# The first gathered token block of a retrieval layer is finished by POOL inside the last quarter of the loop

## What is computed

```python
def peer(h, ...):                       # h: 640 tokens x 1024
    ...                                 # idx, g: 128 chosen experts and gates for each token
    a = gelu(einsum('tkd,td->tk', expert_u[ix], hx))
    return einsum('tk,tkd->td', gx * a, expert_v[ix])
x = x + g2 * peer(h2, ...)
y = rmsnorm(x, final_g)                 # x * rsqrt(mean(x*x) + EPS) * g
```

## Time and profile before

| | |
|---|---|
| median of 3 runs | 1868.1 us (1866.28 to 1871.09) |
| the profiled execution, its time | 1869.13 us |
| the profiled execution, its span | 1867.3 us |
| PE busy | 1732.7 us (93%) |
| DVE busy | 1519.6 us (81%) |
| POOL busy | 797.7 us (43%) |
| ACT busy | 683.2 us (37%) |

### The profile page before, as it was taken

How to read it: one execution, slowest core, us unless ns; L and a number is a source line. 1 busy time by engine, 2 the same in 40 slices (tenths; PEclk the granted TensorE clock), 3 DMA queues, 4 the chain that set the end, 5 groups by cost and what they waited for, 6 DMA issues and landing times.

```text
span 1867.3 us, 29896 instructions
## 1 busy us (share of the span) xinstructions
PE 1732.7 (93%) x9942; PEld 1483.9 (79%) x9942; DVE 1519.6 (81%) x3123; ACT 683.2 (37%) x1135; POOL 797.7 (43%) x646
## 2 busy tenths in 40 slices
PE   5999988889899998499999999999999999999994
PEld 2667656438788888499999999999999999999994
DVE  0732047245989999999999999999999999999997
ACT  1222146101477674233333333333333333333332
POOL 1111000000000000477877778877666666666661
PEclk8999999899999999699999999999999999999997
DMA  9455100700044555799999999999999999999993
GB/s 358 156 198 221 48 1 1 276 39 12 1 91 91 128 115 134 303 394 405 405 400 387 407 407 407 405 402 399 407 406 397 406 404 399 392 402 407 406 405 135
DMA packets 253543, 520.91 MB, mean 279 GB/s; under 512 B 113955, under 2 KB 130979, under 8 KB 252197
## 3 DMA queue, kind: packets, MB, share of 16 engines
q1 hardware_dynamic: 178016, 249.00, 37.4%
q0 software_dynamic: 73728, 268.47, 36.3%
q10 hardware_dynamic: 1734, 2.60, 0.4%
HBM read 488.55 MB, written 31.46 MB: 278 GB/s over the span
## 4 chain that ended last, share of the span: by engine, by line
PE 53%; DVE 24%; issue 13%; DMA 5%; ACT 3%; DVEq 1%; SPq 0%; POOL 0%; POOLq 0%; PEldq 0%; ACTq 0%
DVE arena L1214 11%; PE ps L1594 9%; PE ps L1593 9%; PE ps L1592 9%; PE ps L1512 5%; PE ps L1493 4%; PE ps L1563 4%; DMA arena_w<-in_w_mod 2%; PE ps L1343 2%; DVE V_lo L1164 2%; PE ps L1347 2%; PE ps L1344 2%; DMA U_in<-in_expert_uT 2%; PE ps L1391 1%; DMA arena_w<-in_w_in 1%
## 5 line engine op out<-in xcount | busy, mean ns | idle before, releaser
L1592 PE MATMUL ps<-hT_hi,U_hi 128*128 128x384 f32 x1024 | 344.3, 336 | 13.6 <-DVE U_lo L1159 13.6
L1594 PE MATMUL ps<-hT_hi,U_lo 128*128 128x384 f32 x1024 | 344.5, 336 | 0.0
L1593 PE MATMUL ps<-hT_lo,U_hi 128*128 128x384 f32 x1024 | 343.7, 336 | 0.0
L1592 PE MATMUL ps<-V_hi,C_hi 128*128 128x512 f32 x768 | 300.5, 391 | 18.1 <-DVE C_lo L1189 18.1
L1593 PE MATMUL ps<-V_lo,C_hi 128*128 128x512 f32 x768 | 302.7, 394 | 0.0
L1594 PE MATMUL ps<-V_hi,C_lo 128*128 128x512 f32 x768 | 302.6, 394 | 0.0
L748 ACT CAST V_hi<-V_in 128x1024 fp32r<-128x1024 f32 x128 | 135.0, 1055 | 217.3 <-PE ps L1594 217.3
L1592 PEld LDWEIGHTS ps<-hT_hi,U_hi 128*128 128x128 f32 x1024 | 193.0, 188 | 18.7 <-issue 13.8
L785 ACT ACTIVATE act_t<-ps 128x384 f32<-128x384 f32 x128 | 63.0, 492 | 393.9 <-PE ps L1594 393.9
L479 POOL DMA_INDIRECT arena<-in_expert_u,idxn x128 | 170.4, 1332 | 85.8 <-issue 32.1
L479 POOL DMA_INDIRECT arena<-in_expert_v,idxn x128 | 159.3, 1244 | 93.4 <-DVE arena L1214 42.8
(11 more groups left out here) (239 smaller groups left out, 3218.8 us busy)
## 6 DMA issues: line engine op xcount, KB each, us to landing
U_in<-in_expert_uT SPq DMA_DIRECT2D x128, 512.0 KB, 9.2
V_in<-in_expert_v SPq DMA_DIRECT2D x128, 512.0 KB, 6.4
arena_w<-in_w_mod SPq DMA_DIRECT2D x12, 2048.0 KB, 12.4
gates_scratch<-arena_w SPq DMA_DIRECT2D x6, 4096.0 KB, 20.8
gate_in<-gates_scratch SPq DMA_DIRECT2D x128, 192.0 KB, 7.4
arena_w<-in_w_in SPq DMA_DIRECT2D x4, 2048.0 KB, 8.9
arena_w<-in_w_query SPq DMA_DIRECT2D x1, 7168.0 KB, 21.1
arena_w<-in_w_out SPq DMA_DIRECT2D x2, 2048.0 KB, 10.4
```

The costliest lines, as they stand in the source:

```text
L1592: nc.tensor.matmul(out, hi, rhi, start=start, stop=False)
L1593: nc.tensor.matmul(out, hi, rlo, start=False, stop=False)
L1594: return nc.tensor.matmul(out, lo, rhi, start=False, stop=stop)
```

## The change

Block 4 is taken out of DVE's tail and given to POOL. POOL's gather loop over the last 128 rows is cut in three (two, two and four turns of sixteen rows). After the first part POOL multiplies `accS[:, 0]` by the gate, after the second it adds it to `XF[:, 4]`, and after the last it does the mean and EPS, the power, and two passes for `XF * rstd` and `* fing`. ACT's Square for that block moves to before the loop's last turn. SP waits for the new `s_yfirst` before it writes block 4 and counts the others by `s_y` as before. DVE's `residual(0)` and `norm3(0)` are gone. On PE the last value sums signal once for each of the three token blocks (`s_vend`), and the residual of block b waits for b of them.

```diff
             for n, b in enumerate(FIN):
-                sp.wait_ge(s_y, n + 1)
+                sp.wait_ge(s_y if n else s_yfirst, max(n, 1))
                 sp.dma_start(y[b * P:(b + 1) * P, :], XF[:, b]).then_inc(s_out, 16)
...
-            for n, (table, k) in enumerate(((expert_u, 1), (expert_v, 0), (expert_v, 1))):
+            for n, (table, k) in enumerate(((expert_u, 1), (expert_v, 0))):
                 with pool.Fori(0, SLOTS // 16) as i:
                     sixteen(table, k, i, (n + 1) * SLOTS // RR)
-            for n, b in enumerate(FIN):
+
+            def last_rows(lo, hi):
+                with pool.Fori(lo, hi) as i:
+                    sixteen(expert_v, 1, i, 3 * SLOTS // RR)
+
+            b0, x0, a0 = FIN[0], XF[:, FIN[0]], accS[:, SPARSE.index(FIN[0])]
+            last_rows(0, 2)
+            pool.wait_ge(s_used, 3 * SLOTS)
+            pool.tensor_tensor(a0, a0, G2[:, min(b0, 1), :], ALU.mult).then_inc(s_first, 1)
+            last_rows(2, 4)
+            pool.wait_ge(s_first, 1)
+            pool.wait_ge(s_xf, 16 * NBLK)
+            pool.tensor_tensor(x0, x0, a0, ALU.add).then_inc(s_x2first, 1)
+            last_rows(4, 8)
+            pool.wait_ge(s_sq3first, 1)
+            pool.tensor_scalar(ss[:, b0:b0 + 1], ss[:, b0:b0 + 1], 1.0 / D, EPS, ALU.mult, ALU.add).then_inc(s_first, 1)
+            pool.wait_ge(s_first, 2)
+            pool.tensor_tensor(rstd[:, b0:b0 + 1], ss[:, b0:b0 + 1], powe[:, 0:1], ALU.pow).then_inc(s_first, 1)
+            pool.wait_ge(s_first, 3)
+            pool.wait_ge(s_fing, 16)
+            pool.tensor_scalar(x0, x0, rstd[:, b0:b0 + 1], None, ALU.mult).then_inc(s_first, 1)
+            pool.wait_ge(s_first, 4)
+            pool.tensor_tensor(x0, x0, fing, ALU.mult).then_inc(s_yfirst, 1)
+            for n, b in enumerate(FIN[1:]):
...
                 experts(i, False, False)
+            act.wait_ge(s_x2first, 1)
+            act.activation(accS[:, SPARSE.index(FIN[0])], XF[:, FIN[0]], ACT.Square,
+                           accum_out=ss[:, FIN[0]:FIN[0] + 1]).then_inc(s_sq3first, 1)
             experts(PAIRS - 1, False, True)
-            for n, b in enumerate(FIN):
+            for n, b in enumerate(FIN[1:]):
...
                 else:
-                    dve.wait_ge(s_v, NB1)
+                    dve.wait_ge(s_vend, b)
                     a = tmp2[b - 1]
...
-            residual(0)
             experts(PAIRS - 1, True, add_row(1))
             residual(1)
-            norm3(0)
             for n in range(2, NBLK):
...
                         last = products3(ps[:, 2 + 2 * b + half, :], C_hi[:, j, tok], C_lo[:, j, tok],
                                          V_hi[:, j, col], V_lo[:, j, col], start, stop)
-                last.then_inc(s_v, 1)
+                    if stop:
+                        last.then_inc(s_vend, 1)
+                if not stop:
+                    last.then_inc(s_v, 1)
```

More of the change, by code:

```diff
@@ L313, in program @@
         s_a = sem("s_a"); s_ge = sem("s_ge"); s_c = sem("s_c"); s_chi = sem("s_chi"); s_clo = sem("s_clo")
-        s_v = sem("s_v"); s_h2out = sem("s_h2out"); s_h2in = sem("s_h2in")
+        s_v = sem("s_v"); s_vend = sem("s_vend"); s_h2out = sem("s_h2out"); s_h2in = sem("s_h2in")
         s_row = [sem(f"s_row{i}") for i in range(RR)]
@@ L317, in program @@
         s_x2 = sem("s_x2"); s_sq3 = sem("s_sq3"); s_var3 = sem("s_var3"); s_rstd3 = sem("s_rstd3"); s_y = sem("s_y")
+        s_first = sem("s_first"); s_x2first = sem("s_x2first"); s_sq3first = sem("s_sq3first"); s_yfirst = sem("s_yfirst")
         s_step = sem("s_step"); s_setp = sem("s_setp")
@@ L1225, in residual @@
                 b = FIN[n]
-                if n == 0:
+                if n == 1:
                     dve.wait_ge(s_xf, 16 * NBLK)
@@ L1242, in norm3 @@
                 b = FIN[n]
-                if n == 0:
+                if n == 1:
                     dve.wait_ge(s_fing, 16)
-                dve.wait_ge(s_sq3, n + 1)
+                dve.wait_ge(s_sq3, n)
                 dve.tensor_scalar(ss[:, b:b + 1], ss[:, b:b + 1], 1.0 / D, EPS, ALU.mult, ALU.add).then_inc(s_var3, 1)
-                dve.wait_ge(s_rstd3, n + 1)
+                dve.wait_ge(s_rstd3, n)
                 dve.scalar_tensor_tensor(out=XF[:, b], in0=XF[:, b], scalar=rstd[:, b:b + 1], in1=fing,
```

## The result

The changed kernel takes 1872.8 us (median of 20 runs, 1869.6 to 1875.5) against 1869.5 us for the kernel before (20 runs beside it, 1865.6 to 1872.3). The ratio is 1.0017, 95% interval 1.0011 to 1.0023: some 3.2 us slower, and within 0.3%. The prediction was +4.4 us, also within 0.3%.

What follows compares the result with a forecast made beforehand. The prediction took DVE to bound the kernel, working through from 1608 us to its end. Terms: -2.40 - 2.03 + 8.8 = +4.4 us, 1872.5 us on the median, with a range of 1863.5 to 1876.5 us.

Steps and rivals of the forecast that it cites:

- What bounds the kernel: From 1608 us DVE works through to the end; PE can fall about 3.0 us behind before DVE waits.
- What is taken out: DVE's tail: block-4 residual, 2.40 us, and norm, 2.03 us, both saved in full, together -4.43 us.
- the signal per block: Before DVE's first PSUM residual: without it about 1.0 us of the norm's 2.03 us would be lost.
- What is added: Four POOL passes, two in the last quarter's loop, two behind the last gather, each stopping DVE 2.2 us: 8.8 us.
- The step that decided: From a 128x8 index copy waiting for a DVE instruction: DVE likely can't begin while POOL reads, so full pass charged.
- the one-input pass: Scaling by rstd on POOL behind the last gather, charged to DVE at the full pass, 2.2 us.
- (a): Rival: the four POOL passes run beside DVE and cost it nothing, 1863.7 us; chance 0.17.
- (b): Rival, same four places: longer passes, 3.1 us each, +8.0 us, 1876.1 us; chance 0.21.
- (c): Rival: DVE's back-to-back instructions shut POOL out until gathered rows run out; DVE waits 10.9 us twice, 1889.9; chance 0.07.
- The gathers' margin: In the quarter: next gather leaves some 2.8 us late, lands by 1643.3, DVE wants it at 1646.3; hidden.
- SP's order: SP waits first for POOL's block 4, done about 1841; DVE's first block about 1854.6, hidden by a dozen us.
- The sum: Whole kernel: -2.40 - 2.03 + 8.8 = +4.4 us, 1872.5 us on the median, 0.24%, within 0.3%.

Runs made afterwards that it cites:

- e2: Changed kernel with only the two loop passes on block 4, its norm left out and its residual written; ratio to the kernel before 1.0006.
- e3: Changed kernel without the two loop passes, so only the block-4 work behind the last gather and ACT's Square; ratio to the kernel before 1.0000.
- e4: Changed kernel with the old signal, one for all last value sums; ratio to the kernel before 1.0024.
- e1: Changed kernel with nothing done for block 4, which is written as loaded; ratio to the kernel before 0.9983.
- e6: Changed kernel with eight more one-input POOL passes, one per turn of the last gather loop; ratio to the kernel before 1.0070.
- e8: Kernel before plus signal per block; block-4 norm off DVE (rstd scaling on ACT, final gain on POOL in halves beside PSUM reads), residual on DVE; ratio 0.9991.
- e9: e8 with DVE's tail reordered, each block's mean one step before its scaling; ratio to the kernel before 0.9974, median 1865.9 us.
- e5: Changed kernel with eight more two-input POOL passes, one per turn of the last gather loop; ratio to the kernel before 1.0114.
- e7: Changed kernel with eight more write-only POOL passes (memset), one per turn of the last gather loop; ratio to the kernel before 1.0018.

## Why the prediction was right

**What bounds the kernel.** Right. DVE set the end: e2, e3 and e4 come out to 0.2 to 0.8 us of Q by adding and taking DVE's times (in e4 its wait for PE) alone, and PE's stalls, in size as foreseen (0.4 us behind the first pass, read from two half-steps that took 8.61 and 8.44 us; 1.8 us and then a fallen clock behind the second), cost nothing. What the prediction didn't say is how near PE is on the other side: e1 lost 0.9 us of its saving to it, through V_hi and V_lo. Nor does DVE work through in all of Q: the wait of 0.7 us for `U_hi` lies near 1603 us, just before the 1608 at which its list of waits began.

**What is taken out.** The 4.43 us were there. Of the signal per block it said that about 1.0 us would be lost without it. With the change in place it is 1.7 us. In e4 PE waits 4.5 us before its last sums, which then take 7.2 us at a granted clock of 0.58, where before it waited 1.9 us and took 6.0 at 0.72; DVE asks 0.5 us later than before, by the wait before the last row, which leaves 1.7.

**What is added.** The step that decided, from a 128x8 copy that waits for DVE to a 1024-column pass that stops it, was right, and so was the size of a two-input pass: 2.2 us predicted, 2.19, 2.16 and 2.15 measured. That the size came out so well is luck in part. It was read from a broadcast on POOL, taken at 548 ns and not at the other group's 774, and a two-input pass keeps POOL for 2.5 us and more, not 2.2. The term that was mis-sized is the one-input pass: 2.2 predicted, 0.78 us measured. By the same broadcast it was charged for the time that POOL is busy, which is 3.95 us, while DVE is stopped for a fifth of that. In all the passes cost 7.28 us, not 8.8. Against that stands the 0.51 us wait before the last row, which no row of before could give.

**The rivals.** (a), passes that run beside DVE, falls by the 2.74 us C_lo. (b), longer passes: POOL's records are in fact 2.5 to 3.95 us, all at or over the 2.5 us that the prediction gave as the sign of it, and still each costs DVE 2.2 us or less. That sign was badly chosen: it had to be read on DVE, not on POOL. (c), POOL shut out, falls: the DVE instruction that a two-input pass of the change lengthens begins 0.2 to 0.6 us behind the pass's own start, and the one that the one-input pass lengthens 1.2 us behind it. Its other half, rows that come late, showed only in e6. The gathers' margin held, though one reading in it was wrong: the 0.98 us taken as POOL's idle time is its wait for its own index copy, and it stands behind the pass as well (0.98 us before the gather at 1631.21). SP's order held: POOL has block 4 ready at 1840.3 us and DVE its first block at 1850.8, ten microseconds of room where a dozen were worked out.

**The sum.** +3.4 us of Q instead of +4.4: 1.4 too much for the one-input pass, 0.1 for three two-input ones, 0.5 too little for the wait.

What stays open is the 0.51 us. It stands in every kernel that has the change's DVE program, e1 included, and is absent in before, e8 and e9. The same kernels also share POOL's gather loop cut in three, so the DVE program isn't shown to be the cause. The profile puts the wait down to DVE itself. Fetching of code would be a guess, and the number of transfers on the instruction queue doesn't support it: 28 with the wait, 27 in before and e8, but 28 too in e9, which lacks it. Nothing was tried that would show the cause.

## What to carry to other kernels

Work moved from a saturated DVE to POOL is only gone if the two can run side by side. Where DVE's instructions have two SBUF inputs, a POOL pass that reads SBUF stops DVE, so here two DVE passes of 1.2 us became two POOL passes that cost DVE 2.2 us each. If the move is to pay, put POOL's passes next to DVE instructions that read PSUM, give one-input work to ACT, and leave the rest where it was, as e8 does. When a few microseconds are in question, compare a stretch that both kernels have, and read a contention on the engine that pays, not on the one that causes it.

## What the runs showed of the hardware

A POOL multiply with one input and 1024 columns was slower for POOL than one with two (2.8 to 2.9 us in e6 against 2.4 to 2.6 in e5, beside a busy DVE), and yet stopped DVE for 0.83 us against 2.20 beside a C_lo, and for 1.38 against 2.74 beside a V_lo that had begun 0.45 us before. A POOL memset of the same size took 0.97 us and stopped nothing (e7). A DVE instruction with one input in PSUM and one in SBUF kept its 1.22 us beside a two-input POOL pass, and the 512 columns of that pass then took 1.26 to 1.29 us (e8, e9). POOL's small index copies of 128x8 lasted 0.19 to 1.15 us; in each of the two kernels 62 of the 64 ended 0.04 to 0.05 us behind the end of a DVE instruction.
